# The sixteen gate1 chunks: from VectorE multiply-adds to column-tiled matmuls ahead of the score steps

## The reference, cut to what matters

```python
c_act = jax.nn.silu(c)
mod = (c_act @ w_mod[l] + b_mod[l])[:, None, :]
sh1, sc1, g1, sh2, sc2, g2 = jnp.split(mod, 6, axis=-1)
h = rms_norm(x, norm1_g[l]) * (1.0 + sc1) + sh1
(fq, fk, fv, ff, nq, kc, vc, ksl, vsl, kwn, vwn, ng, ca, cg) = split_in(h @ w_in[l])
...
mixed = jnp.concatenate([o_fox, o_nsa, o_conv], axis=-1)
x = x + g1 * (mixed @ w_out[l])
h = rms_norm(x, norm2_g[l]) * (1.0 + sc2) + sh2
x = x + g2 * (jnp.square(jax.nn.relu(h @ w_mlp1[l])) @ w_mlp2[l])
```

## Time and profile before

| | |
|---|---|
| time, median of 3 runs | 1207.67 us (1206.52 to 1208.06) |
| span of the profiled execution | 1208.7 us |
| PE busy | 1155.1 us, 96% of the span |
| PE weight load busy | 1004.8 us, 83% |
| DVE busy | 898.4 us, 74% |
| ACT busy | 607.4 us, 50% |
| DMA | 306 MB, 253 GB/s over the span |

### The profile page before, as it was taken

One profiled execution on the slowest core, in us unless ns is written; L12 is line 12 of the kernel. 1 busy time (PEld: TensorE's weight loads), 2 busy tenths in 40 slices (PEclk: granted clock), 3 DMA queues, 4 the chain that ended last, 5 costly groups with the idle time before them and its releaser, 6 DMA issues.

```text
span 1208.7 us, 17358 instructions
## 1 busy us (share of the span) xinstructions
PE 1155.1 (96%) x6811; PEld 1004.8 (83%) x6811; DVE 898.4 (74%) x1025; ACT 607.4 (50%) x886; POOL 10.5 (1%) x29
## 2 busy tenths in 40 slices
PE   4998999999989998999999999999999999999996
PEld 4898988988877776999788888888888888888785
DVE  5998989988889979996865666545666545667675
ACT  6655447876755546544433444433444333444452
POOL 2000000000000000000000000000000000000000
PEclk7998999989999999999999999999999999999999
DMA  9999996547847786886666665556665556655441
GB/s 375 419 420 420 421 370 249 175 163 277 282 175 276 284 325 244 341 350 249 219 240 238 249 237 191 192 179 237 245 233 183 186 196 244 237 214 188 160 174 69
DMA packets 46329, 306.11 MB, mean 253 GB/s; under 512 B 6381, under 2 KB 8249, under 8 KB 9785
## 3 DMA queue, kind: packets, MB, share of 16 engines
q1 hardware_dynamic: 44304, 302.58, 66.6%
q10 hardware_dynamic: 1896, 2.64, 0.7%
q0 software_dynamic: 64, 0.02, 0.0%
HBM read 303.10 MB, written 2.12 MB: 253 GB/s over the span
## 4 chain that ended last, share of the span: by engine, by line
PE 72%; DVE 12%; DMA 7%; ACT 5%; issue 4%; SPq 0%; ACTq 0%; DVEq 0%
PE quad L1102 14%; PE quad L1116 11%; PE quad L1117 11%; PE quad L1118 11%; PE quad L1104 8%; DMA mod_raw<-in_w_mod 4%; PE quad L1092 4%; PE quad L1094 4%; PE quad L1093 4%; DVE w_lo L1592 3%; DVE mod_raw L1599 2%; ACT w_hi L768 2%; ACT score L831 1%; DMA first_raw<-in_w_mod 1%; ACT conv_p L808 1%
## 5 line engine op out<-in xcount | busy, mean ns | idle before, releaser
L1592 DVE TENSOR_TENSOR w_lo<-raw,w_hi 128x1024 fp32r<-128x1024 f32 (+1 forms) x372 | 446.3, 1208 | 247.6 <-ACT w_hi L768 246.9
L768 ACT ACTIVATE w_hi<-raw 128x1024 fp32r<-128x1024 f32 (+1 forms) x372 | 387.6, 1046 | 428.7 <-PE quad L1118 222.7
L1102 PE MATMUL quad<-act,w_hi 128*128 128x512 f32 x768 | 266.4, 390 | 0.0
L1092 PE MATMUL quad<-act,w_hi 128*128 128x256 f32 x760 | 218.0, 287 | 9.4 <-DVE w_lo L1592 7.1
L1104 PE MATMUL quad<-act,w_lo 128*128 128x256 f32 x768 | 216.6, 282 | 0.0
L1093 PE MATMUL quad<-act,w_hi 128*128 128x256 f32 x760 | 215.6, 284 | 0.0
L1094 PE MATMUL quad<-act,w_lo 128*128 128x256 f32 x760 | 215.4, 283 | 0.0
L1116 PE MATMUL quad<-w_hi,u_hi 128*128 128x512 f32 x496 | 196.7, 397 | 0.6 <-DVE u_lo L2061 0.6
L1118 PE MATMUL quad<-w_hi,u_lo 128*128 128x512 f32 x496 | 196.2, 396 | 0.0
L1117 PE MATMUL quad<-w_lo,u_hi 128*128 128x512 f32 x496 | 196.1, 395 | 0.0
L1102 PEld LDWEIGHTS quad<-act,w_hi 128*128 128x128 f32 x768 | 144.2, 188 | 30.3
(11 more groups left out here) (307 smaller groups left out, 1175.3 us busy)
## 6 DMA issues: line engine op xcount, KB each, us to landing
raw<-in_w_main SPq DMA_DIRECT2D x184, 1024.0 KB, 4.8
mod_raw<-in_w_mod SPq DMA_DIRECT2D x72, 1024.0 KB, 6.6
first_raw<-in_w_mod SPq DMA_DIRECT2D x14, 1024.0 KB, 14.7
late_raw<-in_w_mod SPq DMA_DIRECT2D x10, 1024.0 KB, 8.3
x_a<-in_x SPq DMA_DIRECT2D x2, 1024.0 KB, 7.2
x<-in_x SPq DMA_DIRECT2D x2, 1024.0 KB, 8.6
bias_t<-bias_scratch ACTq DMA_DIRECT2D x1, 1536.0 KB, 14.8
raw<-in_w_tail SPq DMA_DIRECT2D x4, 352.0 KB, 8.3
```

The lines of the kernel that those rows point to most:

```text
L768: A(dst[:, 0:2 * width], block_half(raw, j, width), ACT.Copy).then_inc(hi_done, 1)
L1092: mm(out, hi, act_hi[:, k, :], start=begin and m % 2 == 0, stop=False, skip_group_check=True)
L1102: mm(out, w_hi[j % 4][:, cols], act_both[:, k, :, :].rearrange("p h t -> p (h t)"), start=begin, stop=False, skip_group_check=True)
L1592: TTn(lo[:, 0:2 * width], block_half(raw, j, width), hi[:, 0:2 * width].bitcast(f32), ALU.subtract)\
```

## The change

The `g1` chunks are no longer used as rows of `w_mod` but as blocks: chunk n holds all 2048 inputs of outputs 128n to 128n + 127, laid out so that the 128 columns of each of 16 input tiles stand side by side. PE multiplies a chunk ahead of the scores of an even step (`gate_block`): 16 float32 matmuls with a stationary operand of 128 by 32 (one column of `c_act`, repeated) and 128 moving columns, each written to one of four 32-partition groups of the bank that the scores use, in its last 128 columns. DVE adds the 128 by 128 result to `acc[1]` right behind the bias (`gate_sum`), and with that the buffer is free. The sum over partitions stays as it was, with `ones_conv` (1/512) and a scale of 16 in the copy. The table now has two kinds of chunks: the FoX steps 0, 2, 4, 6, 8, 10 and the NSA steps 0, 2, 4 (two), 6, 8, 10, 12, 14, 16 carry the 16 blocks, the columns stand in the turns before and at the odd NSA steps from 7 to 23. The bias row is now written to 32 partitions of `acc[1]` instead of one.

```diff
-MODS_AT = {turn: 1 + (turn in (9, 21, 27, 33)) for turn in range(5, 60, 2) if turn != 45}
-MODS_AT |= {FOX_AT + AHEAD + t: 1 for t in (1, 3, 5, 6, 7, 9, 11)}
-MODS_AT |= {NSA_TURN + t: 1 for t in (0, 1, 4, 7, 9, 13, 14, 15, 17, 18, 19, 20, 21, 23)}
-MODS_AT |= {NSA_TURN + t: 2 for t in (5, 11)}
+MOD_PLAN = {turn: COLUMN * (1 + (turn in (9, 21, 27, 33))) for turn in range(5, 60, 2) if turn != 45}
+MOD_PLAN |= {FOX_AT + AHEAD + t: GATE for t in (0, 2, 4, 6, 8, 10)}
+MOD_PLAN |= {NSA_TURN + t: GATE for t in (0, 2, 6, 8, 10, 12, 14, 16)} | {NSA_TURN + 4: GATE * 2}
+MOD_PLAN |= {NSA_TURN + t: COLUMN for t in (7, 9, 11, 13, 15, 17, 19, 21, 23)}
...
-                pool.dma_start(a[0:1, :], bmod_d[s:s + 1, :]).then_inc(acc_init[s], 16)
+                rows = (32, 1)[s]
+                pool.dma_start(a[0:rows, :], bmod_d[s:s + 1, :].to_broadcast([rows, D])).then_inc(acc_init[s], 16)
...
-            def scores(first):
+            def gate_block(m):
+
+                n = GATE_MODS.index(m)
+                src, full, arrivals = mod_buffer(m)
+                pe.wait_ge(full, arrivals)
+                for k in range(KT):
+                    rows = slice(32 * (k % 4), 32 * (k % 4 + 1))
+                    last = mm(head_bank[n % 2][rows, 3 * P:4 * P], c_act[:, k:k + 1].to_broadcast([P, 32]),
+                              src[:, k * P:(k + 1) * P], start=k < 4, stop=k >= KT - 4, skip_group_check=True)
+                last.then_inc(pe_block, 1)
+
+            def scores(first, gates):
...
+                for m in gates:
+                    gate_block(m)
...
-            def transposes(a):
+            def transposes(a, gates):
                 pe.wait_ge(p_ready, a + 1)
+                if gates:
+                    pe.wait_ge(mod_step, gates[-1] + 2)
...
+            def gate_sum(m):
+
+                n = GATE_MODS.index(m)
+                if n == 0:
+                    dve.wait_ge(acc_init[0], 16)
+                dve.wait_ge(pe_block, n + 1)
+                cols = slice(n * P, (n + 1) * P)
+                TTn(acc[1][:, cols], acc[1][:, cols], head_bank[n % 2][:, 3 * P:4 * P], ALU.add).then_inc(mod_step, 1)
```

More of the change, by code:

```diff
@@ L166 @@
 MOD_FIRST = 8
-MOD_G1 = 2 * KT
-MOD_H2 = 3 * KT
 MOD_G2 = 5 * KT
-MODS_AT = {turn: 1 + (turn in (9, 21, 27, 33)) for turn in range(5, 60, 2) if turn != 45}
-MODS_AT |= {FOX_AT + AHEAD + t: 1 for t in (1, 3, 5, 6, 7, 9, 11)}
-MODS_AT |= {NSA_TURN + t: 1 for t in (0, 1, 4, 7, 9, 13, 14, 15, 17, 18, 19, 20, 21, 23)}
-MODS_AT |= {NSA_TURN + t: 2 for t in (5, 11)}
-MOD_LATE = 64
+COLUMN, GATE = "c", "g"
+MOD_PLAN = {turn: COLUMN * (1 + (turn in (9, 21, 27, 33))) for turn in range(5, 60, 2) if turn != 45}
+MOD_PLAN |= {FOX_AT + AHEAD + t: GATE for t in (0, 2, 4, 6, 8, 10)}
+MOD_PLAN |= {NSA_TURN + t: GATE for t in (0, 2, 6, 8, 10, 12, 14, 16)} | {NSA_TURN + 4: GATE * 2}
+MOD_PLAN |= {NSA_TURN + t: COLUMN for t in (7, 9, 11, 13, 15, 17, 19, 21, 23)}
+MOD_LATE = 64
+MODS = [(turn, kind) for turn in sorted(MOD_PLAN) for kind in MOD_PLAN[turn]]
+MODS_AT = {turn: len(MOD_PLAN[turn]) for turn in MOD_PLAN}
+GATE_MODS = [MOD_FIRST + i for i, (_, kind) in enumerate(MODS) if kind == GATE]
+GATES_AT = {turn: [MOD_FIRST + i for i, at in enumerate(MODS) if at == (turn, GATE)] for turn in MOD_PLAN}
+COLUMN_MODS = [m for m in range(MOD_G2) if m not in GATE_MODS]
+assert len(GATE_MODS) == KT
 MOD_SLOT = {m: m % 4 for m in range(8, 20)} | {m: (m - 20) % 3 for m in range(20, 28)}
@@ L1387, in _ @@
                     if scored is not None:
-                        scores(scored)
+                        scores(scored, GATES_AT.get(slot + AHEAD, ()))
                     if transposed is not None:
-                        transposes(transposed)
-                        transposes(transposed + 1)
+                        transposes(transposed, GATES_AT.get(slot + AHEAD - 1, ()))
+                        transposes(transposed + 1, ())
                 if slot == 2:
@@ L1597, in modulation_column @@
                 dve.wait_ge(full, arrivals)
[L1598 removed]
+                col = COLUMN_MODS.index(m)
                 v.tensor_tensor_reduce(out=src[:, :], in0=src[:, :], in1=acc[0][:, :], scale=1.0, scalar=0.0,
@@ L1601, in modulation_column, with modulation_row @@
                     .then_inc(mod_step, 1)
-            def modulation_row(m, k, gate, src, full, arrivals, first=False):
+            def modulation_row(m, k, src, full, arrivals, first=False):
                 dve.wait_ge(full, arrivals)
                 if first:
-                    dve.wait_ge(acc_init[gate], 16)
+                    dve.wait_ge(acc_init[1], 16)
                 dve.wait_ge(mod_step, m + 1)
-                out = acc[1 - gate][:, :]
+                out = acc[0][:, :]
                 STT(out, src[:, :], c_act[:, bass.ds(k, 1)], out, ALU.mult, ALU.add).then_inc(mod_step, 1)
             def later_modulation(m):
[L1613 to L1616, removed]
-                    modulation_column(m, *source)
+                if m not in GATE_MODS:
+                    modulation_column(m, *mod_buffer(m))
+            def gate_sum(m):
[5 more added lines that the diff above has]
+                TTn(acc[1][:, cols], acc[1][:, cols], head_bank[n % 2][:, 3 * P:4 * P], ALU.add).then_inc(mod_step, 1)
             def scale_shift(first, count, done, gain, at):
@@ L1893, in _ @@
                         bias_scores(scored + 1)
+                        for n in GATES_AT.get(turn, ()):
+                            gate_sum(n)
                     if summed is not None and summed % 4 == 2:
@@ L2236 @@
     w_h2, b_h2 = by_column(sh2, sc2)
+    w_g1 = mod[:, g1].reshape(KT, P, KT, P).transpose(2, 1, 0, 3).reshape(KT, P, D)
+    w_columns = np.concatenate([w_h1, w_h2])
+    w_mod_first = np.stack([w_g1[GATE_MODS.index(m)] if m in GATE_MODS else w_columns[COLUMN_MODS.index(m)]
+                            for m in range(MOD_G2)])
     names = ["fq", "fk", "fv", "f", "nq", "kc", "vc", "ks", "vs", "kw", "vw", "ng", "ca", "cg"]
```

11 lines of the change are left out of this document (6 added, 5 removed).

## The result

| | before | after |
| --- | --- | --- |
| median of 4 runs, us | 1207.9 (1206.5 to 1208.2) | 1223.6 (1221.2 to 1225.2) |
| span of the profiled execution, us | 1208.7 | 1221.8 |

The change makes the kernel slower: the ratio is 1.0132, 95% interval 1.012 to 1.0144, or 15.8 us by the medians and 13.1 us by the two profiled executions. The forecast was 1220.2 us, range 1211 to 1235. Time and direction came out as forecast; most terms of the sum did too. Three did not: the opening, one stretch of half clock that nothing in the prediction asked for, and a first fall of the clock that went away entirely.

What follows compares the result with a forecast made beforehand. The prediction took PE as the bound, DVE close behind. From the 1208.7 us span, +0.6 +14.9 -10.5 -0.9 -3.3 -1.5 +11.2 +2.0 gave 1221.2; with the median 1.0 below, 1220.2 us, range 1211 to 1235.

Steps and rivals of the forecast that it cites:

- The bound and DVE's relief: Attention: PE bound; DVE delays gone except at the first FoX step, -10.5; `mix_n` wait, -0.9; two later clock falls, -3.3 us.
- The first clock fall: First FoX step: the block shortens the wait from 2.7 to 1.7 us; half of 3.0 us half-clock cost saved, -1.5.
- Price and number of the blocks: PE ahead of scores: 14 blocks at 1.0 us and one at 0.85, the first hidden in a wait, +14.9 us.
- B: Blocks on PE: starts keep program order, 1.9 us a block, 13.5 us more, 1233.7 us; chance 0.11.
- C: Blocks on PE: no overlap with 32-column operands, 3.6 us a block, 39 us more, 1259.2 us; chance 0.04.
- Refill waits: NSA steps 8, 10, 14 and 16: PE waits 2.6, 6.5, 0.5 and 1.6 us for chunks to land, +11.2 us.
- Clock behind the 6.5 us wait: After the wait at NSA step 10: half clock follows, +2.0 us, ends 1.6 and 3.0.
- The opening: Bias row written to 32 partitions, 256 KB more while DMA is full at 420 GB/s, +0.6 us.
- From the span to the median: Last step: the median stands 1.0 us below the profiled span, so 1221.2 becomes 1220.2 us.

Runs made afterwards that it cites:

- Experiment 4: Kernel before, DVE's work on the 25 chunks of the attention stretch cut to one column each, no blocks on PE: 1192.9 us.
- Experiment 8: Kernel before, with the 24 narrow products of the compressed scores issued twice: 1210.8 us.
- experiment 5: Two edits to the changed kernel: every block multiplied twice, 1237.5 us; four matmuls in a row for each column group, 1240.5 us (one run).
- first two kernels of experiment 6: Changed kernel with the gate's bias written to one partition, 1220.4 us (one run); the same with GpSimd scaling that row by 32 later, 1220.6 us.
- experiment 1: Changed kernel with the refill of a block's buffer issued ahead of the raw load in turns with a block: 1216.0 us.
- experiment 3: Changed kernel with another plan of turns and the refill ahead of the raw load in turns with a block, bias row in 32 partitions: 1208.5 us.
- the one-row versions: Gate's bias written to one partition instead of 32: in the changed kernel 1220.4 (one run) and, scaled later, 1220.6 us; with other turns and refill first 1205.6 us.
- the third kernel of 6: Changed kernel with the bias still written to 32 partitions, but by GpSimd at 184 us instead of in the opening: 1222.7 us.
- the second kernel of 5: Changed kernel with a block's 16 matmuls written four in a row for each column group instead of going round the groups: 1240.5 us (one run).

## Why the prediction was right, step by step

- **The bound and DVE's relief** (-10.5, -0.9, -3.3). Right. Experiment 4 gives 15.0 us by medians for what I had at 14.7. In the kernel after DVE's bias starts 0.03 us behind the modelled end of PE's scores in most steps; the largest lateness in NSA is 1.3 us at step 18, which PE's half hides.
- **The first clock fall** (-1.5, half of 3.0). It went away entirely: with the block in the wait, 1.7 us of waiting brought no half clock at 246 us, in this kernel or in any with the blocks. I had no row for it, and the ends 0 and -3.0 held it. Its size is uncertain: it lasted 6.8 us in the profile before but 3.4 in experiments 4 and 8, where the program is the same up to there.
- **Price and number of the blocks** (+14.9). Right: 0.81 us of starts and 0.20 to the scores, 1.01 us, and 0.87 for the second of a pair. The row of two groups told what four would do. The rule of the Trainium skill that I had weighed ("TensorE: Matmul & The Clock Gate", Part 3: matmuls keep the program's order) would have made 1.9 us of it; 16 starts in 0.4 us contradict it, and experiment 5 shows the limit that remains. Rivals B and C fall; yet the price hangs on the order in which the block is written, and with four matmuls in a row for each group it is 2.39 us, above B's.
- **Refill waits** (+11.2). Right in place and cause: forecast 2.6, 6.5, 0.5 and 1.6 at steps 8, 10, 14 and 16, measured 1.6, 6.6, 1.1 and 1.1, 10.3 in all. Step 8 came shorter since half clock had slowed PE on the way (2.3 us in the first two kernels of experiment 6, without it), step 14 longer since its load took 5.3 us to land with others on their way (the term that I took at 4.7 us). Experiments 1 and 3 take the waits away by what was named as their cause.
- **Clock behind the 6.5 us wait** (+2.0). It fell at 381.9 and stayed low to 388.8; 4.8 us of work lie in that, 2.4 us lost.
- **Missing: half clock from 354.6 to 361.5** (about +1.8 for what lies ahead of step 6's score; what lies behind it only shortened the wait at step 8). I had looked for falls behind waits alone. Experiment 8 points at the narrow stretch.
- **The opening** (+0.6). Mis-sized. By the two first profiles it was +0.5 (first score less its block 240.05 against 239.58), but the one-row versions give 3.0 us back by medians. The half clock at 112 to 119 us hid part of the cost in the pair of first profiles: 6.8 us of it in the kernel before, 3.4 in the kernel after. Where it is 6.8 us in both, the first score less its blocks is at 239.4 to 239.9 without the early write (the kernel before, experiments 4 and 8, the third kernel of 6) and at 240.7 and 241.5 with it (experiment 3, the second kernel of 5). Counting bytes at 420 GB/s was the step that failed: the write slowed the others' loads while it lasted and delayed the one chunk that DVE waited for.

By the two profiles: 0.5 + 14.9 - 10.5 - 0.9 - 3.3 - 3.0 + 10.3 + 2.4 + 1.8 = +12.2, of 13.1 measured. Two things behind attention are not in it: the kernel before waits 0.7 us for `nsa_lo` at 440.8 us and the kernel after does not, and the kernel after runs at half clock from 474.1 to 477.5, right behind the wait for `w_lo`, where the kernel before does not.

**From the span to the median.** This step was wrong. I put the median 1.0 us below the profiled span, because it was so in the kernel before. But in every execution on record, of every kernel, the time is 1.8 to 2.0 us above its own span; for the changed kernel too, 1223.65 against 1221.8. So the profile before was taken in a slow execution: its span of 1208.7 stands for some 1210.6 us (an estimate), 2.7 above the median and above the slowest one on record (1210.4). Against that profile the forecast of +12.5 was 0.6 us short of the 13.1 measured; the other 2.7 us up to the 15.8 of the medians are this step. That the sum came within 0.6 us owes something to luck: the missing stretch of half clock (+1.8) and the first fall (-1.5 more than forecast) nearly cancel.

## What to carry to other kernels

When work moves to an engine that takes it in order ahead of everything else, what feeds it moves too: count from the moment its buffer comes free, through every load ahead in the same queue, to the moment it is wanted, for each place, also for those that a repair creates. Give a buffer that must be refilled four turns rather than two and put its load ahead of loads that wait for something later: both were needed, neither sufficed (waits of 3.6 and 9.7 us left by each alone, none by both, 15.1 us gained). And price the exchange without its waits first: 15 us taken off the waiting engine for 15 us put on the bound one leaves nothing to win but what falls into an idle gap.

## What the hardware showed that I had not expected

- Four column groups of 32 run side by side at no loss when the program goes round them: 32 float32 instructions started within 0.81 us. With eight in a row for each group they started over 2.19 us, each next group's first one overtaking only three.
- PE fell to half clock (1.2 GHz) while busy without a break, in or right behind a stretch of narrow instructions: 10.2 us of it when 24 such products were made 48. The Trainium skill ("TensorE: Matmul & The Clock Gate", Part 1) ties the clock to how busy PE has been; that it is busy in the profile's sense was not enough here.
- A 256 KB write from one row to 32 partitions through GpSimd's queue went with 310 to 361 GB/s of DMA instead of 413 to 421 for 5 us, at the same busy share; leaving it to one row gained 3 us.
- The same kernel varied by more than 7 us from run to run in one case (experiment 1, 1211.2 to 1218.5); its profiled execution, the fastest, had a short stretch of half clock in attention, 3.4 us. A single profile of a kernel with waits near such a fall can stand several us from its median: the one before stood some 2.7 us above. Compare each profile's own time with the median before taking terms from it.
